# Compression weights loaded with the first ones, and the end of attention without a barrier: a two-layer hybrid decoder on one core

## The reference, cut to what matters

```python
def _compress(k, pos_emb, w1, w2):
    ...
    first = jnp.einsum('bcsgd,sdh->bcgh', ch + pos_emb[None, None, :CMP_STRIDE, None, :], w1[:CMP_STRIDE])
    second = jnp.einsum('bcsgd,sdh->bcgh', ch + pos_emb[None, None, CMP_STRIDE:, None, :], w1[CMP_STRIDE:])
    hid = jax.nn.silu(first[:, :-1] + second[:, 1:])
    return jnp.einsum('bngh,hd->bngd', hid, w2)

def _merge(x, ya, za, yb, zb, g_mix, p_i, w_out_a, w_out_b, w_o, w_ple, w_ple_gate):
    br_a = jnp.einsum('btc,cd->btd', jax.nn.silu(za) * ya, w_out_a)
    br_b = jnp.einsum('btc,cd->btd', jax.nn.silu(zb) * yb, w_out_b)
    ...
```

## Time and profile before

| | |
|---|---|
| median of 3 runs | 2536.3 us (2535.97 to 2537.24) |
| profiled execution | 2534.94 us, its span 2533.2 us |
| PE busy | 2377.4 us (94% of the span) |
| DVE, ACT, POOL busy | 1249.4, 993.8, 196.3 us |
| mean granted TensorE clock | 0.98 of full speed |
| longest chain | PE 78%, SP's queue 7%, DVE 6%, ACT 3%, DMA 3% |

### The profile page before, as it was taken

One profiled execution on the slowest core, in us unless ns is written; L12 is line 12 of the kernel. 1 busy time (PEld: TensorE's weight loads), 2 busy tenths in 40 slices (PEclk: granted clock), 3 DMA queues, 4 the chain that ended last, 5 costly groups with the idle time before them and its releaser, 6 DMA issues.

```text
span 2533.2 us, 45635 instructions
## 1 busy us (share of the span) xinstructions
PE 2377.4 (94%) x17997; PEld 2073.3 (82%) x17997; DVE 1249.4 (49%) x2336; ACT 993.8 (39%) x2029; POOL 196.3 (8%) x335
## 2 busy tenths in 40 slices
PE   5999999998999999989989999999899998997996
PEld 4999999996788655569979999999877884554996
DVE  4444222454675566564464432234557556555535
ACT  4222222434554455532332221243447445554222
POOL 0000000000000123310000000000000003332000
PEclk9999999998999999989989999999999999999998
DMA  5343255618552666672243334546374509667521
GB/s 177 118 142 124 84 155 139 141 36 155 67 67 34 91 106 110 97 233 93 75 150 133 119 105 123 149 107 137 41 148 67 67 9 142 101 101 166 167 76 44
DMA packets 292987, 278.58 MB, mean 110 GB/s; under 512 B 92536, under 2 KB 281272, under 8 KB 291366
## 3 DMA queue, kind: packets, MB, share of 16 engines
q1 hardware_dynamic: 288358, 238.81, 43.3%
q0 software_dynamic: 4416, 36.85, 3.9%
HBM read 248.72 MB, written 43.53 MB: 115 GB/s over the span
## 4 chain that ended last, share of the span: by engine, by line
PE 78%; SPq 7%; DVE 6%; ACT 3%; DMA 3%; issue 2%; DVEq 1%; POOL 1%; ACTq 0%
PE ps L734 45%; PE ps L924 11%; PE ps L850 7%; SPq L546 4%; PE ps L1171 2%; DVE chL L1899 2%; PE ps L877 2%; DMA k_win<-in_state_win 2%; SPq L520 2%; PE ps L1049 1%; PE ps L949 1%; ACT chH L1478 1%; PE ps L1073 1%; PE ps L1034 1%; SPq L536 1%
## 5 line engine op out<-in xcount | busy, mean ns | idle before, releaser
L734 PE MATMUL ps<-hH,wH 128*128 128x272 f32 x2048 | 426.2, 290 | 17.7 <-DVE hL L1751 17.7
L406 DVE TENSOR_TENSOR wL<-w_raw,wH 128x2048 fp32r<-128x2048 f32 (+2 forms) x112 | 253.3, 2261 | 382.0 <-ACT wH L397 377.6
L734 PE MATMUL ps<-hH,wL 128*128 128x272 f32 x2048 | 427.4, 290 | 0.0
L734 PE MATMUL ps<-hL,wH 128*128 128x272 f32 x2048 | 424.4, 289 | 0.0
L734 PEld LDWEIGHTS ps<-hH,wH 128*128 128x128 f32 x2048 | 323.9, 189 | 21.1 <-issue 16.3
L734 PEld LDWEIGHTS ps<-hH,wL 128*128 128x128 f32 x2048 | 323.0, 190 | 0.0
L734 PEld LDWEIGHTS ps<-hL,wH 128*128 128x128 f32 x2048 | 322.8, 189 | 0.0
L1478 ACT ACTIVATE chH<-ps 64x256 fp32r<-64x256 f32 x512 | 207.2, 405 | 241.0 <-PE ps L924 232.4
L1899 DVE TENSOR_TENSOR chL<-ps,chH 64x256 fp32r<-64x256 f32 x512 | 216.6, 423 | 172.7 <-ACT chH L1478 165.1
L397 ACT ACTIVATE wH<-w_raw 128x2048 fp32r<-128x2048 f32 (+2 forms) x112 | 211.0, 1884 | 87.0 <-PE ps L734 77.6
L704 POOL TENSOR_SCALAR pr<-pr,inv,zg 128x512 f32<-128x512 f32 (+3 forms) x256 | 158.0, 627 | 1019.8 <-DVE inv L2091 1019.6
(11 more groups left out here) (291 smaller groups left out, 3774.0 us busy)
## 6 DMA issues: line engine op xcount, KB each, us to landing
w_raw<-in_w_in SPq DMA_DIRECT2D x60, 1024.0 KB
craw<-in_cache_kv SPq DMA_DIRECT2D x256, 128.0 KB, 5.2
w_raw<-in_w_in SPq DMA_DIRECT2D x64, 256.0 KB
k_sel<-in_cache_kv SPq DMA_DIRECT2D x128, 128.0 KB, 5.6
v_sel<-in_cache_kv SPq DMA_DIRECT2D x128, 128.0 KB, 6.6
out_new_win_sample<-in_state_win POOLq DMA_DIRECT2D x16, 1016.0 KB, 5.8
w_raw<-in_w_out_a SPq DMA_DIRECT2D x8, 1024.0 KB
k_win<-in_state_win SPq DMA_DIRECT2D x16, 512.0 KB, 7.3
```

Of the source, the lines that this page charges most:

```text
L406: dve.tensor_tensor(block_part(wL, b), block_part(w_raw, b), block_part(wH, b).bitcast(F32), ALU.subtract).then_inc(w_lo, 1)
L734: last = nc.tensor.matmul(ps[:, bank + hf, 0:HALF], st, x[:, k, hf * HALF:(hf + 1) * HALF], start=k == 0 and w is wH and x is xH, stop=k = ...
```

## The change

**1.** The two `w2` DMAs move on SP: from behind the pages of n = 2 to right behind `w1` of the keys, ahead of the fifth `B_TM` block. `w2` gets a place of its own behind `w1_raw`, in the memory of `m`.

**2.** The barrier at the end of attention goes; PE, ACT, DVE and SP wait for single semaphores. `zbs` and the first output block are loaded once the last pair's keys are transposed (`sa_kt`), right behind the last pair's values, and not after `s_fin`; `m` once the last scores are out.

**3.** Seven of the eight gate products (their 512 prompt columns) go to POOL, ahead of its scaling for unit 58; the sample columns of all eight are one DVE instruction at unit 61; the eighth product stays on DVE after the last unit. The parts `bH`, `bL` lie where `qT` and `yT` were, so that slice 0 can be split before the last unit is over.

**4.** The first output block's weights are split in `sample_step(7)` on both engines.

```diff
-        w2 = at("w2", [P, 2, 2, HD], 75136)
+        w2 = home("w2", [P, 2, 2, HD], M0 + 16384)
...
                         load_w1(l, "cmp_w1_k")
+                        for kv, name in enumerate(("cmp_w2_k", "cmp_w2_v")):
+                            sp.dma_start(w2[:, kv], a[name][ds(l, 1)].rearrange("l (k p) d -> p (l k) d", p=P)).then_inc(w2_in, 16)
...
                 load_pages(l, 2)
-                for kv, name in enumerate(("cmp_w2_k", "cmp_w2_v")):
-                    sp.dma_start(w2[:, kv], a[name][ds(l, 1)].rearrange("l (k p) d -> p (l k) d", p=P)).then_inc(w2_in, 16)
...
-                sp.wait_ge(s_fin, 4 * l + 4)
...
+                sp.wait_ge(sa_kt, 48 * l + 48)
                 load_ob(0)
-                sp.dma_start(zbs[:, 0:4], a["zb_keep"][l, 0:4].rearrange("k p t -> p k t")).then_inc(zb_back[0], 16)
-                sp.dma_start(zbs[:, 4:8], a["zb_keep"][l, 4:8].rearrange("k p t -> p k t")).then_inc(zb_back[1], 16)
+                sp.dma_start(zbs[:], a["zb_keep"][l].rearrange("k p t -> p k t")).then_inc(zb_back, 16)
+                sp.wait_ge(s_fin, 4 * l + 4)
                 load_ob(1)
                 sp.dma_start(gb[:], a["gb_keep"][l].rearrange("k p t -> p k t")).then_inc(gb_back, 16)
-                phase_over(sp, l, 0)
+                sp.wait_ge(pa_s, UNITS * (l + 1))
                 sp.dma_start(m[:], a["m_keep"][l]).then_inc(m_back, 16)
...
                 for i in range(UNITS):
                     n, at_u = P * (unit(i)[2] + 1), UNITS * l + i
+                    if i == 58:
+                        pool.wait_ge(zb_back, 16 * l + 16)
+                        pool.wait_ge(pa_o, 8 * l + 7)
+                        for c in range(KT - 1):
+                            pool.tensor_tensor(zbs[:, c, 0:SEQ], zbs[:, c, 0:SEQ], yT[:, c, 0:SEQ], ALU.mult).then_inc(a_p, 1)
...
                 output(UNITS - 1)
-                end_phase(pe, l, 0)
...
+                    if front is None:
+                        act.wait_ge(sa_s, 12 * l + 12)
+                        make_high(act, l, B_OB)
...
-                    if i == 61:
-                        make_high(act, l, B_OB)
+                    if i == UNITS - 1:
+                        act.wait_ge(a_p, 7 * l + 7)
+                        act.wait_ge(a_s, l + 1)
+                        a_high(0)
                 turned(UNITS - 1)
                 put_out(UNITS // 8 - 1)
-                end_phase(act, l, 0)
...
+                    if front is None:
+                        make_low(dve, l, B_OB)
...
-                    if i == 62:
-                        make_low(dve, l, B_OB)
+                    if i == 61:
+                        dve.wait_ge(zb_back, 16 * l + 16)
+                        dve.drain()
+                        dve.tensor_tensor(zbs[:, :, SEQ:TOK], zbs[:, :, SEQ:TOK], yT[:, :, SEQ:TOK], ALU.mult).then_inc(a_s, 1)
...
+                a_low(0)
                 turned(UNITS - 1)
-                end_phase(dve, l, 0)
...
                 a_low(1)
-                a_product(2)
-                a_product(3)
-                for c in range(4, KT):
-                    a_low(c - 2)
-                    a_product(c)
-                a_low(6)
-                a_low(7)
+                a_low(2)
+                dve.wait_ge(pa_o, 8 * l + 8)
+                dve.tensor_tensor(zbs[:, KT - 1, 0:SEQ], zbs[:, KT - 1, 0:SEQ], yT[:, KT - 1, 0:SEQ], ALU.mult).then_inc(a_f, 1)
+                for c in range(3, KT):
+                    a_low(c)
```

More of the change, by code:

```diff
@@ L271, in build @@
         k_sel, v_sel = home("k_sel", [P, 2, HC, KV], F0), at("v_sel", [P, 2, HC, KV], H_L)
-        k_win, v_win = (at(n, [P, 2, 4, KV], o) for n, o in (("k_win", 0), ("v_win", 8192)))
-        skT = at("skT", [P, 4, 512], 16384)
-        spT = at("spT", [P, 16, P], 24576)
-        ssel = at("ssel", [P, PAST + NSAM], 32768)
-        swsc = at("swsc", [P, WIN + NSAM], 36992)
-        pc = at("pc", [P, 4, 64], 39168)
-        sy = at("sy", [P, P], 40192)
-        snew = at("snew", [P, 4, 2, NSAM], 40704)
+        k_win, v_win = (at(n, [P, 2, 4, KV], o) for n, o in (("k_win", 0), ("v_win", 8448)))
+        skT = at("skT", [P, 4, 512], 16640)
+        spT = at("spT", [P, 16, P], 25344)
+        ssel = at("ssel", [P, PAST + NSAM], 33536)
+        swsc = at("swsc", [P, WIN + NSAM], 37760)
+        pc = at("pc", [P, 4, 64], 39936)
+        snew = at("snew", [P, 4, 2, NSAM], 41472)
+        sy = at("sy", [P, P], 135296)
         zbs = home("zbs", [P, KT, TOK], F0)
         gb = at("gb", [P, KT, TOK], H_L)
-        mH = at("mH", [P, KT, TOK], R_Z, F32R)
-        mL = at("mL", [P, KT, TOK], H_H, F32R)
+        bH = at("bH", [P, KT, TOK], R_Z, F32R)
+        bL = at("bL", [P, KT, TOK], H_H, F32R)
+        mH = at("mH", [P, KT, TOK], R_A, F32R)
+        mL = at("mL", [P, KT, TOK], R_A + 17408, F32R)
         pin = at("pin", [P, 5, PLE], H_L)
@@ L1267, in _ @@
                 output(UNITS - 1)
-                end_phase(pe, l, 0)
                 def slot_free(s):
-                    if 4 <= s < 12:
+                    if s == 3:
+                        pe.wait_ge(pa_o, 8 * l + 8)
+                        pe.wait_ge(sa_ys, 4 * l + 4)
+                    elif 4 <= s < 12:
                         pe.wait_ge(ob_free, 8 * l + s - 3)
@@ L1287, in _ @@
                     if s == 0:
-                        fm_tile(b, 0, 0, aH, aL, parts=a_lo, first=8 * l + 1)
+                        fm_tile(b, 0, 0, bH, bL, parts=a_lo, first=8 * l + 1)
                     else:
-                        fm_tile(b, s % 2, 2 * (s % 4), aH, aL)
+                        fm_tile(b, s % 2, 2 * (s % 4), bH, bL)
                 for s in range(8, 16):
@@ L1313, in _ @@
                         if i + q == 0:
-                            fm_tile(b, 0, bank, aH, aL, parts=xo_lo, first=8 * l + 1)
+                            fm_tile(b, 0, bank, bH, bL, parts=xo_lo, first=8 * l + 1)
                         else:
-                            fm_tile(b, q % 2, bank, aH, aL)
+                            fm_tile(b, q % 2, bank, bH, bL)
                     b = B_PL + 3 * i + 2
@@ L1367, in _ @@
                 square(0, c)
[L1368 removed]
+            end_phase(act)
             make_high(act, 0, 0)
@@ L1646, in sample_exp, with a_high @@
                     act.drain().then_inc(sa_e, 1)
+                def a_high(c):
+                    act.activation(bH[:, c, :], zbs[:, c, :], ACT.Copy).then_inc(a_hi, 1)
                 for i in range(1, UNITS):
@@ L1662, in _ @@
                         sample_exp(sample_block(mm)[1], 1, swsc)
-                    if i == 61:
-                        make_high(act, l, B_OB)
+                    if i == UNITS - 1:
+                        act.wait_ge(a_p, 7 * l + 7)
+                        act.wait_ge(a_s, l + 1)
+                        a_high(0)
                 turned(UNITS - 1)
                 put_out(UNITS // 8 - 1)
-                end_phase(act, l, 0)
-                def a_high(c):
-                    act.wait_ge(a_f, 8 * l + c + 1)
-                    act.activation(aH[:, c, :], zbs[:, c, :], ACT.Copy).then_inc(a_hi, 1)
-                a_high(0)
-                a_high(1)
-                for c in range(2, KT):
+                for c in range(1, KT - 1):
                     a_high(c)
+                act.wait_ge(a_f, l + 1)
+                a_high(KT - 1)
                 for i in range(4):
@@ L1687, in _ @@
                         act.wait_ge(wo_done, 8 * l + c + 1)
-                        act.activation(aH[:, c, :], xT[:, c, :], ACT.Copy).then_inc(xo_hi, 1)
+                        act.activation(bH[:, c, :], xT[:, c, :], ACT.Copy).then_inc(xo_hi, 1)
                 for c in range(2):
@@ L1742, in _ @@
             dve.drain()
-            end_phase(dve, 0, -1)
+            end_phase(dve)
             make_low(dve, 0, 0)
```

37 lines of the change are left out of this document (15 added, 22 removed).

## The result

The changed kernel takes 2509.5 us in the median of 4 runs (2505.9 to 2513.8), the one before 2536.8 (2536.0 to 2543.3): a ratio of 0.9888, 95% interval 0.9865 to 0.9910. 2505.8 us were forecast, in a range of 2497 to 2518. The profiled execution took 2509.95 us (span 2508.2), 25.0 us less than that of before, where 30.5 were forecast. The kernel before scattered far more in later runs than in its first three: 2532.5 to 2545.5 us over some fifty. A difference of 2 us between two kernels is therefore no finding by itself.

What follows compares the result with a forecast made beforehand. PE bounds the kernel, so only its stands and half-clock time can be won. 25.7 us from the compression plus 4.8 from the end of attention, 30.5 off 2534.9, gave 2504.4; the median lies 1.4 higher: 2505.8 us, range 2497 to 2518.

Steps and rivals of the forecast that it cites:

- Step 1: Compression: loading w2 about 90 us earlier removes PE's wait and the slow matmuls behind it, 25.7 us for both layers.
- the air for n = 3: Compression, layer 0: the last n = 3 pages land at 633.2, PE takes them at 634.1, so 0.9 us to spare.
- Step 2: End of attention: seven POOL products at 1.23 us each make turn(58) 6.9 us late, 5.2 after some comes back.
- nearly 1 us for landing: Allowance added to the 8.3 us transfer of output block and zbs, putting the landing of zbs at 1077.5.
- the 1.7 us that should come back at `turn(59)`: End of attention: with DVE's inv ready, turn(59) follows turn(58) by 2.13 us instead of 3.84.
- Step 3: End of attention: splitting the output weights earlier, in idle ACT and DVE time, gives back 2.9 us at unit 62.
- Step 4: Output tiles: without the barrier the first tile ends 8.2 us after the last output, not 12.4; 4.2 us gained.
- T: End of the last attention output; forecast 1.8 us late per layer, at 1101.8, counting half the gain of full clock.

Runs made afterwards that it cites:

- e1: The kernel before with only the early w2 load added, end of attention as before: 2511.4 us, ratio 0.9897.
- e5: The changed kernel without GpSimd's seven gate products (left out of the result), its wait for zbs kept: 2497.5 us, ratio 0.9837.
- e6: As e3 (products on VectorE), with zbs loaded later, behind the scores of unit 60; second output block and gb also later: 2498.7 us, ratio 0.9839.
- e7: As e3, with the first output weights split back at units 61 and 62, as in the kernel before: 2513.9 us, ratio 0.9904.
- e11: As e6, but products and high parts begin only behind the copy of the last output: 2505.1 us, ratio 0.9875.
- e2: The changed kernel with the w2 loads back in their old place, the new end of attention kept: 2534.6 us, ratio 0.9993.
- e3: The changed kernel with the seven products on VectorE behind the last unit, one between two low parts: 2506.5 us, ratio 0.9867.
- e4: The changed kernel with the seven GpSimd products spread: one behind each scaling of units 58 to 62, two behind that of 63: 2504.2 us, ratio 0.9869.
- e9: As e6, with zbs also loaded, needlessly, at the early place; VectorE waits for the second load: 2499.4 us, ratio 0.9853.
- e8: As e6, with three of the seven products on GpSimd behind its last scaling: 2497.6 us, ratio 0.9838.
- e10: As e6, with the w2 loads back in their old place: 2519.2 us, ratio 0.9933.
- e12: As e6, with the second output block and gb loaded ahead of zbs, only zbs waiting for unit 60's scores: 2511.1 us, ratio 0.9889.

## Why the prediction held, and where its sizes were off

**Step 1, 25.7 us: right.** e1 alone gives 25.6, and the traces of e1 and of the changed kernel have 26.8. The four matmuls of `w2` come without a wait and the clock stays full. PE waits for no pages in the changed kernel, but the air for n = 3 was thinner than the 0.9 us that were counted: the last of them, issued at 626.4 and landing up to 6.5 us later, were there at 632.9 at the latest for 633.4, and in e1 PE waited 0.47 us for them.

**Step 2, the products: right in kind, somewhat small.** The price was right to the digit (1.23 us, with the second input counted as much as the first), and so nearly was the landing (1078.8 for 1077.5). 5.2 us net a layer were forecast, and e5 shows 6.0. Two terms are off. `zbs` landed 1.3 us later than forecast, for which the sum had a row of the transfer (8.3 us) but none for its "nearly 1 us for landing"; the products start with the landing, so this is the 1.1 to 1.2 us by which `turn(58)` was later than said in the two layers. And the 1.7 us that should come back at `turn(59)` did not (3.89 us behind `turn(58)`): POOL has that unit scaled in time, but PE does its work between the two turns at half clock. Without the products the landing costs PE nothing: unit 58 is scaled 0.5 us later than in e6, and `turn(58)` no later.

The lock between the two engines works also as a delay of VectorE: a 128x2 operation of 0.16 us takes 1.04 and 1.25 us beside a product. The Trainium skill ("SBUF — State Buffer", "Who interferes with whom") says that such a `tensor_scalar` can go into a mode with both port pairs and then waits for the whole GpSimd instruction; the trace agrees, since 1.25 us is one product long. Here it was hidden, POOL being the one waited for.

**Step 3, the split, 2.9 us a layer: right in kind, 2.4 at its place.** 5.0 us from `turn(61)` to `turn(62)` became 2.64. e7 gives 3.7 a layer in the median and 4.5 in its trace, of which 2.1 are half clock behind the place; this the step did not have.

**Step 4, no barrier, 4.2 us a layer: right.** e11, which undoes most of it, costs 3.2 to 4.6 by the medians and 2.1 by the trace; there the tiles of the kernel that it is compared with also wait 0.2 us a slice for VectorE's products, so it is not the full worth of the step. In the profile after, the last output ends at T = 1093.2. The chain of waits has the tiles without a gap from slice 3 on:

```profile
1096.38 0.65 DVE bL L2276
1097.03 0.04 issue
1097.07 6.94 PE ps L740 x53
```

The 30 matmuls of the slices 3 to 7 take 6.94 / 53 = 0.131 us each, so the first tile ends at 1097.07 + 3.9 = 1101.0, T + 7.8. 8.2 were forecast, and 12.4 it was before: 4.6 us gained.

**The sum.** Per layer the pieces measured singly are +6.0 - 3.7 - 3.2 = -0.9 us, and the whole gives -1.2 (e2) and -0.95 (the changed kernel against e1), where -2.4 was forecast. Each piece is uncertain by some 3 us a layer, so that they add up so well is partly luck; the traces have -1.1 and -1.7 (the changed kernel) and -2.0 and -2.1 (e2). The term that was mis-sized is T, "1.8 us late". With the shift of 10.5 taken out, layer 0 is 8.1 us late at `turn(58)` (forecast 6.9), 8.2 at `turn(59)` (5.2), 6.0 at `turn(62)` (2.3) and 3.7 at T (1.8): the late landing and the half clock added 3.0 us up to `turn(59)` and 0.7 up to `turn(62)`, and the full clock at the very end gave 1.8 back, which the forecast had counted at half. With -1.0 to -1.2 us a layer in place of -2.4 the forecast would have been 2508 to 2509; 2509.5 were measured. Part of the closeness is luck: the forecast started from an execution of before without half clock in layer 0's attention.

**What the forecast did not have** is that stand: PE without a releaser for 0.6 to 2.5 us, in layer 0 near 1066 and in layer 1 near 2293, in both layers of every kernel that loads `zbs` early and once (the changed one, e2, e3, e4, e5, e7), in layer 0 of e9, and at this place never in the seven kernels that don't (before, e1, e6, e8, e10, e11, e12). In the changed kernel it is hidden under the wait for POOL; it costs where nothing waits for POOL. From ahead of it to `turn(58)` e3 loses 1.7 us in layer 0 and 6.7 in layer 1, e7 1.6 and 6.6, e6 nothing.

The stand is always ahead of the same matmul of its layer, and in all fourteen kept traces one packet of the instruction queue comes shortly before that matmul. Where PE stands it goes on 1.2 to 1.5 us behind the end of that packet. The packet itself takes no longer there (1.06 to 1.11 us) than elsewhere (0.96 to 1.47), but it starts later: with 51 matmuls to go or fewer, mostly none to 14, where without a stand it starts with 71 to 131 to go. In the 2 us ahead of it the queues move 395 to 412 GB/s in all fourteen cases of an early `zbs` (seven kernels, two layers), of which thirteen have the stand, and 0 to 197 GB/s in the fourteen others, of which none has. The queues of the changed kernel from 2291 to 2293 us, a window in which the data of `zbs` are running out, and of before at the same place of the program, from 2310 to 2312:

```profile
DMA packets 241, 0.51 MB, mean 257 GB/s; under 512 B 11, under 2 KB 11, under 8 KB 240
...
q8 instruction: 1, 0.02, 3.4%
```

```profile
DMA packets 1, 0.02 MB, mean 8 GB/s; under 512 B 0, under 2 KB 0, under 8 KB 0
...
q8 instruction: 1, 0.02, 3.0%
```

The Trainium skill ("Advanced Engine Details and Errata", "ISA Cache") says that an engine's code comes in lines of 256 instructions, 16 KB each; the packets of 0.02 MB agree with that size. The queue moves 143 of them, which would be 36,608 instructions, an estimate by that page; PE has 17,997 matmuls and as many weight loads, so they fit PE's code. That the stand is a wait for code, and that the code starts late because the queues are full, is supported by this, by e6 (2 of 2 stands gone) and in part by e9 (1 of 2 back), not proved: e9's layer 1 has the traffic and no late packet. The size fits the traces: e6 is 7.8 us faster than e3, which loses 8.4 us at the stands and in the half clock behind them, and e9 with one stand is 0.7 slower than e6, where its trace loses 1.4. By the medians alone e3 and e6 are not clearly apart (their intervals overlap slightly).

## What to carry to other kernels

An idle engine on the critical handover is not free room: GpSimd had 9 us to spare, but the data came at the end of them, so each us of work put there was a us on PE's path (6.0 us a layer for 8.6 us of work). With the same products on VectorE, behind the last unit where PE's next tile can start on the first slice, and with `zbs` loaded later, the end of attention gave 17 us by itself (e10) and not 2.4 (e2); how much of that each of the two gives is not separated by the medians. The best version measured, e8 (2497.6 us) with e6 next to it (2498.7), is 11 to 12 us faster than the change and 39 to 40 faster than before.

A load can be too early as well as too late. Here issuing `zbs` at the first moment when its place was free filled the queues when PE's next code was due, and PE stood in 13 of 14 cases; issuing it behind two others (e12) made it late; behind the scores of unit 60 and ahead of the others it cost nothing.

## What the runs showed of the hardware that was not expected

- PE stood for up to 2.51 us for no reason that a semaphore shows, and went on 1.2 to 1.5 us behind the end of a 16 KB packet of the instruction queue that had started late, behind 395 to 412 GB/s of data.
- The granted clock falls to half for some 3 to 7 us at single places of the attention in some executions and not in others, at equal work and equal traffic: 1.00 and 0.55 at 938 to 945 us in before and e2. Eleven of the fourteen traces have it somewhere in layer 0's attention. Most of the scatter of 4 to 13 us between runs of one kernel is likely this; it was not separated from other causes.
- A 128x2 `tensor_scalar` on VectorE took 1.25 us in place of 0.16 beside a GpSimd product, and three GpSimd products beside VectorE's subtractions 1.40 us in place of 1.23.
